# Four edits in the first attention of a three-block transformer kernel: the place of the dilated outputs, the way of the dilated values, the place of the norms, and four early gate tiles

## The reference

```
proj = h @ w_in[l]                       # h: rms_norm, scaled and shifted by c
qa, ka, va, qb, kb, vb, gates = split(proj)
qa, ka = rms_norm per head
o_a = neighbourhood_attention(qa, ka, va, rpb)        # 8 heads of 64
qb, kb = partial_rotary(rms_norm per head)
for g, (win, dil) in enumerate(((128,1),(512,4),(2048,16))):   # 3 groups of 4 heads
    o_g, lse_g = dilated_window_attention(qb[g], kb[g], vb[g], win, dil)
o_b = sum_g softmax(lse)[g] * o_g
gate_a, gate_b = split(sigmoid(gates + b_gate))
merged = gate_a * (o_a @ w_proj_a) + gate_b * (o_b @ w_proj_b)
x = x + gt1 * (merged @ w_o)
x = x + gt2 * swiglu(...)
```

## Time and profile before

| | |
|---|---|
| median of 3 runs | 3040.32 us |
| profiled execution | 3041.17 us |
| its span | 3038.6 us |
| mean granted clock | 0.958 of 2.4 GHz |
| PE busy | 2692.9 us, 89% |
| DVE, ACT, POOL busy | 1535.9, 1026.3, 1294.6 us |
| HBM traffic | 259 MB read, 3.15 MB written |

### The profile page before, as it was taken

The page is one execution under the profiler, slowest core; times in us unless marked ns, Lnnn a source line. Parts: engine busy times, 40 slices in busy tenths (PEclk is TensorE's granted clock), DMA queues, the critical chain, the costliest instruction groups (busy, mean ns, idle before and its releaser), DMA issues. The chain is left out here.

```text
span 3038.6 us, 37066 instructions
## 1 busy us (share of the span) xinstructions
PE 2692.9 (89%) x14304; PEld 2183.0 (72%) x14304; DVE 1535.9 (51%) x2279; ACT 1026.3 (34%) x1739; POOL 1294.6 (43%) x654
## 2 busy tenths in 40 slices
PE   1799669989999788888789999998799999699998
PEld 1587447868888565665578888886787888578886
DVE  2423424655445524555675555555577686632223
ACT  2333323232222433333431221113455555432222
POOL 2335554444444445555623333333344444344443
PEclk9899879999999899999999999998899999799999
DMA  5423222433334200000023333331111111022221
GB/s 193 150 93 114 98 79 101 148 125 130 132 133 138 69 29 15 25 18 15 35 98 124 119 125 112 118 111 53 49 42 63 43 56 49 35 83 97 97 97 70
DMA packets 78526, 264.53 MB, mean 87 GB/s; under 512 B 8464, under 2 KB 12688, under 8 KB 78352
## 3 DMA queue, kind: packets, MB, share of 16 engines
q1 hardware_dynamic: 70416, 248.67, 23.4%
q10 hardware_dynamic: 7648, 12.19, 1.3%
q0 software_dynamic: 288, 1.31, 0.1%
HBM read 258.99 MB, written 3.15 MB: 86 GB/s over the span
## 5 line engine op out<-in xcount | busy, mean ns | idle before, releaser
L1916 POOL TENSOR_TENSOR SLO<-RAW,SHI 128x1024 fp32r<-128x1024 f32 (+1 forms) x336 | 816.0, 2430 | 1215.7 <-ACT SHI L1754 1215.6
L1754 ACT ACTIVATE SHI<-RAW 128x1024 fp32r<-128x1024 f32 (+1 forms) x336 | 346.5, 1034 | 1199.9 <-PE PS L2175 1166.1
L2173 PE MATMUL PS<-HLh,SHI 128*128 128x512 f32 x1680 | 686.6, 409 | 24.3 <-DVE HLl L1985 15.2
L2174 PE MATMUL PS<-HLl,SHI 128*128 128x512 f32 x1680 | 659.6, 393 | 0.0
L2175 PE MATMUL PS<-HLh,SLO 128*128 128x512 f32 x1680 | 659.2, 392 | 0.0
L2173 PEld LDWEIGHTS PS<-HLh,SHI 128*128 128x128 f32 x1680 | 318.6, 190 | 118.4 <-issue 41.7
L2173 PE MATMUL PS<-hh,SHI 128*128 128x512 f32 (+1 forms) x944 | 352.8, 374 | 19.3 <-DVE hl L2065 9.9
L2175 PEld LDWEIGHTS PS<-HLh,SLO 128*128 128x128 f32 x1680 | 317.9, 189 | 69.1
L2174 PEld LDWEIGHTS PS<-HLl,SHI 128*128 128x128 f32 x1680 | 319.2, 190 | 65.2 <-issue 7.5
L2174 PE MATMUL PS<-hl,SHI 128*128 128x512 f32 (+1 forms) x944 | 347.0, 368 | 0.0
L2175 PE MATMUL PS<-hh,SLO 128*128 128x512 f32 (+1 forms) x944 | 346.9, 367 | 0.0
(11 more groups left out here) (227 smaller groups left out, 3957.0 us busy)
## 6 DMA issues: line engine op xcount, KB each, us to landing
RAW<-in_k_w SPq DMA_DIRECT2D x316, 512.0 KB, 3.2
ADA<-in_k_w SPq DMA_DIRECT2D x132, 512.0 KB, 4.1
early<-in_k_w SPq DMA_DIRECT2D x12, 512.0 KB, 10.7
RAW<-in_k_w SPq DMA_DIRECT2D x20, 256.0 KB, 2.7
XL<-in_xT ACTq DMA_DIRECT2D x1, 2048.0 KB, 12.4
bi<-in_k_bias ACTq DMA_DIRECT2D x16, 128.0 KB, 2.2
out<-XL SPq DMA_DIRECT2D x8, 256.0 KB, 2.1
bi<-in_k_bias ACTq DMA_DIRECT2D x8, 192.0 KB, 3.2
```

The costliest lines, as they stand in the source:

```text
L1754: eng.activation(u.hi, u.w, ACT.Copy).then_inc(S["a_hi"], 1)
L1916: eng.tensor_tensor(u.lo, u.w, u.hi.bitcast(F32), ALU.subtract).then_inc(S["g_lo"], 1)
L2173: eng.matmul(st.out, lh, rh, start=st.first and j == 0, stop=False)
L2174: eng.matmul(st.out, lh, rl, start=False, stop=False)
```

## The change

1. The dilated outputs of group j = 0 lie in XC behind c1 (high and low part), those of j = 1 on c1; only the latter wait for tile 47 (`[mtok(0, 47)] if j else []`).
2. The dilated values are computed with tokens side by side (`lhs_nat`), written to a scratch tensor in HBM (`v4`), and read back with every fourth token on its place (`dl_turned`, one job or two later). Both DMAs go out on ScalarE's queue; the values' token is now that of the read.
3. The tails of q and k start one yield later, and mark themselves as emitted two yields later.
4. Four gate tiles of the merge's first column pair (`early_gate`) stand at the end of the dense list: a projection and a copy to an f cell. The f ring changes places with pt, so that those cells stay untouched while the merge's buffers are laid out. In the merge, for p = 0, the sigmoid reads the copy.

In the diff, line numbers of the kernel after are up to 37 higher than those of the profile.

```diff
--- before.py
+++ after.py
@@ -834,15 +834,15 @@
 
     W = arena({"va": (1, 4 * 512, F32, 4), "qa": (4, 512, F32, 4), "vb": (1, 3 * 4 * 256, F32, 4),
                "qb": (6, 512, F32, 4), "mk": (1, 1536, F32, 4), "bi": (5, 384, F32, 4), "e": (4, 384, F32, 4),
-               "pt": (2, 768, F32, 4), "f": (4, 512, F32, 4), "r": (2, 512, F32, 4),
+               "f": (4, 512, F32, 4), "pt": (2, 768, F32, 4), "r": (2, 512, F32, 4),
                "m": (8, 8, F32, 4)}, [])
     qb2 = [place(f"qb2_{i}", [128, 512], F32, AR + 2048 * i)[:, :] for i in range(6)]
     oah = place("oah", [128, 4 * NT], F32R, HCh_at)
     oal = place("oal", [128, 4 * NT], F32R, HCl_at)
-    obh = place("obh", [128, 2 * NT], F32R, XC_at)
-    obl = place("obl", [128, 2 * NT], F32R, XC_at + 4096)
+    obs = [[place(f"ob{n}{j}", [128, NT], F32R, XC_at + (4096, 0)[j] + 2048 * i)[:, :] for i, n in enumerate("hl")]
+           for j in range(2)]
     oa = [(oah[:, NT * k:NT * k + NT], oal[:, NT * k:NT * k + NT]) for k in range(4)]
-    ob = [(obh[:, NT * k:NT * k + NT], obl[:, NT * k:NT * k + NT]) for k in range(2)]
+    ob = [tuple(o) for o in obs]
     oa_rdy, ob_rdy = [[] for _ in range(4)], [[] for _ in range(2)]
     MK = W["mk"].cells[0].ap
     stage = place("mstage", [128, 4224], F32, AR)
@@ -915,9 +915,6 @@
     def lhs_nat(i, k):
         return hl[k][0][:, 128 * i:128 * i + 128], hl[k][1][:, 128 * i:128 * i + 128], hl_rdy[k]
 
-    def lhs_dl(i, k):
-        return hl[k][0][:, i:NT:4], hl[k][1][:, i:NT:4], hl_rdy[k]
-
     qa_cells, qb_cells = {}, {}
 
     def na_qk(j, which):
@@ -930,10 +927,12 @@
 
         def tail():
             views = ("p (c r) -> p c r", "p (r c) -> p c r")
+            yield
             c.rdy = [headnorm(sq, b, b.ap, t, NT, gq8 if which == "q" else col("gka"), W, c.ap, c.free, views)]
             qa_cells[(which, j)] = c
+            yield
+            yield
             emitted.add(f"{which} {j}")
-            yield
 
         yield
         return tail()
@@ -994,6 +993,20 @@
 
     vb = W["vb"].cells[0].ap.rearrange("p (g t n) -> p g t n", g=3, t=4)
     vb_tok = []
+    v4 = [nc.dram_tensor(f"v4_{g}", [NT, 256], F32, kind="Internal").ap() for g in range(3)]
+    v4_tok = {}
+
+    def dl_values(g):
+
+        toks = []
+        yield from vproj("w_in", 1536 + 1536 + 256 * g, 4, lhs_nat, lambda i: vb[:, g, i, :], toks, vn_read)
+        v4_tok[g] = dma("act", v4[g].rearrange("(t p) n -> p t n", p=128), vb[:, g], toks)
+
+    def dl_turned(g):
+
+        vb_tok.append(dma("act", vb[:, g], v4[g].rearrange("(p t) n -> p t n", t=4), v4_tok[g]))
+        return
+        yield
 
     def dl_qk(j, g, which):
         u = getunit("w_in", ktiles(0, 8), seg((1536 if which == "q" else 1536 + 768) + 256 * g + 128 * j, 128))
@@ -1058,13 +1073,30 @@
     def dl_make(it, b, t_mm):
         j, r = it["j"], it["r"]
         ob_rdy[j] += out_split(b, t_mm, b.ap[:, 0:128], ob[j][0][:, r:NT:4], ob[j][1][:, r:NT:4],
-                               [mtok(0, 47)])
+                               [mtok(0, 47)] if j else [])
 
     for g in range(3):
         for w_ in ("q", "k"):
             qb_cells[(w_, g, 0)] = W["qb"].cells[2 * g + (w_ == "k")]
 
     run(bgz(pipelined([na_qk(0, "q"), na_qk(0, "k")])))
+    gated = {}
+
+    def gate_proj(m, off, W):
+        u = getunit("w_in", ktiles(0, 8), seg(3840 + 128 * (off + m), 128))
+        b = take()
+        t, = yield from proj(u, 0, [(b.ap, hl, hl_rdy, b.free)])
+        release(u, t)
+        return b, t, W["f"].next()
+
+    def early_gate(q, off):
+
+        b, t, sg = yield from gate_proj(q, off, W)
+        t1 = tick("a_vcopy")
+        put(VCopy("a", sg.ap, b.ap, t, sg.free, t1))
+        give(b, t1)
+        gated[(q, off)] = (sg, t1)
+        yield
 
     def qb2_cells():
         na_done = all_now()
@@ -1081,12 +1113,14 @@
     dense = []
     for j in range(1, 4):
         dense += [after(f"na {j - 2} scored")] if j > 1 else []
-        dense += [na_qk(j, "q"), na_qk(j, "k")]
-        g = j - 1
-        dense += [vproj("w_in", 1536 + 1536 + 256 * g, 4, lhs_dl, lambda i, g=g: vb[:, g, i, :], vb_tok, vn_read)]
-    dense += [dl_qk(0, g, w) for g in range(3) for w in "qk"]
+        dense += [na_qk(j, "q")]
+        dense += [dl_turned(j - 2)] if j > 1 else []
+        dense += [na_qk(j, "k"), dl_values(j - 1)]
+    dense += [dl_qk(0, 0, "q"), dl_turned(2), dl_qk(0, 0, "k")]
+    dense += [dl_qk(0, g, w) for g in (1, 2) for w in "qk"]
     dense += [after("na 3 done"), qb2_cells()]
     dense += [dl_qk(1, g, w) for g in range(3) for w in "qk"]
+    dense += [early_gate(q, off) for q in range(2) for off in (0, 8)]
     dense += [some(bg, 32)]
     first_out = lambda it, b, t: (na_make if "t" in it else dl_make)(it, b, t)
     weave((attention(heads, W, first_out), 0.6), (bgz(pipelined(dense)), 1.0))
@@ -1105,14 +1139,17 @@
             for q in range(2):
                 for off in (0, 8):
                     m = 2 * p + q
-                    u = getunit("w_in", ktiles(0, 8), seg(3840 + 128 * (off + m), 128))
-                    b = take()
-                    t, = yield from proj(u, 0, [(b.ap, hl, hl_rdy, b.free)])
-                    release(u, t)
-                    sg = W["f"].next()
+                    b = None
+                    if p == 0:
+                        sg, t = gated[(q, off)]
+                        src = sg.ap
+                    else:
+                        b, t, sg = yield from gate_proj(m, off, W)
+                        src = b.ap
                     t1 = tick("a_gate")
-                    put(Gate(b.ap, sg.ap, col("bg", off + m), t, sg.free, t1))
-                    give(b, t1)
+                    put(Gate(src, sg.ap, col("bg", off + m), t, sg.free, t1))
+                    if b:
+                        give(b, t1)
                     sgs[(q, off)] = (sg, t1)
                     yield
             for off, src, nk, o, ord_ in ((0, "w_proj_a", 4, oa, oa_rdy), (8, "w_proj_b", 2, ob, ob_rdy)):
```

## The result

The changed kernel takes 2996.64 us (median of 4 runs, 2988.56 to 3000.66), the kernel before 3040.0 in the same comparison: ratio 0.985, interval [0.983, 0.988]. It is 43.4 us faster; 77 were forecast. 2996.6 lies 3.6 us outside the range of 2948 to 2993. Two single executions of later runs, 7911 us (e4_gates) and 9089 us (best_w50_7), are left out of every median here. The profiled execution took 2998.94 us, of which 2994.7 is the span.

A forecast was written before the change was run, and what follows sets the result against it. TensorE, busy 89% of the span, was taken to bound the kernel. Gains less costs summed to 77.1 us, taking 3041.2 us to 2964.1, stated as 2964, with a range from 2948 to 2993.

The forecast's parts named there:

- (1): First dilated group: outputs beside c remove TensorE's 25.69 us stall; gain 26.5 us, bounds 20 and 30.
- (2): Dilated value projections: 288 matmuls with side-by-side weights gain 32.8 us; round trips cost 0, less cover 2 us.
- (3): Attention's q and k norms, further from scores: waits shortened by 6, 3.3 and 2 us, clock gain 5 us.
- (4): Second dilated group: four gate tiles fill TensorE's waits; gain 8.5 us, bounds 3 and 14.
- (5): Merge's start: TensorE waits 3.3 us for a late weight split; cost 5 us, bounds 0 and 9.
- behind the merge: Work after the merge: same order but for some coefficient tiles, none forced in a row; 0 us.
- three terms of waits: Attention norms: scores waiting for `qa` gain 6 us, head sums waiting for squares 3.3, first head sum of q 2.
- fourth term of (3): Attention: shorter waits leave less TensorE work at half clock; gain 5 us, bounds 0 and 7.
- term for less cover: Attention: shorter value projections leave less work between a score and its transposes; cost 2 us, bounds 0 and 15.
- (A): Rival: value projections get no shorter; 2997 us, or 2980 with half of the gain; chance 0.14.
- (D): Rival: the forced run of coefficient tiles only moves to the second dilated group; 25 us return, 2989 us; chance 0.02.
- signs set out for a wrong forecast: Value projections' pace over 0.2 us, TensorE's attention waits over 45 us, or clock from 120 us to merge under 0.85.

The follow-up runs named there:

- e4_gates: Kernel before with only the four gate tiles moved into the second dilated group; 3042.42 us, ratio 0.9998.
- best_w50_7: Changed kernel with six PSUM banks, read-back in the next job, sigmoids at their products, attention share 0.5, coefficient tile every 7th merge step; 2965.74 us.
- e2_values: Kernel before with only the dilated values from side-by-side weights, turned through HBM; 3021.96 us, ratio 0.9935.
- e3_norms: Kernel before with only the tails of q and k starting one step later and marked two later; 3041.83 us, ratio 0.9995.
- b_before: Kernel before with six PSUM banks in rotation instead of four until the last neighbourhood scores, nothing else; 3038.42 us, ratio 0.9986.
- b_norms: Kernel before with the later tails of q and k and six PSUM banks in rotation instead of four; 3025.56 us, ratio 0.994.
- a_less_norms: Changed kernel without the later tails of q and k (norms as before); 3002.84 us, ratio 0.987.
- b_banks: Changed kernel with six PSUM banks in rotation instead of four until the last neighbourhood scores; 2984.31 us, ratio 0.981.
- n_trip: Changed kernel without the six DMAs of the round trips through HBM, so part of the result differs; 2995.38 us.
- m1_turned: Changed kernel with each read-back from HBM issued at the head of the next projection's job, not in an empty job; 2993.93 us, ratio 0.9835.
- e1_outputs: Kernel before with only the first dilated group's outputs beside c, without the wait for coefficient tile 47; 3020.35 us, ratio 0.993.

## Why the prediction was wrong, step by step

| step | forecast | alone | inside the changed kernel |
|---|---|---|---|
| (1) outputs beside c | 26.5 | 23.0 | |
| (2) values | 32.8 - 2 | 23.2 | |
| (3) norms, with the clock's 5 | 16.3 | 2.3 | 6.5 |
| (4) gates in the second group | 8.5 | 7.0 | 8.4 |
| (5) merge's start | -5 | -8.6 | -7.4 |
| behind the merge | 0 | | -7.0, again -5.3 |

The first four rows are attention stretches: of the edit alone against before, or of the changed kernel without the edit against it (324.5 - 318.0 and 326.4 - 318.0). They were forecast at 82.1 us and gave 57.3. The column "alone" holds for (2) and (3) the shorter stall too, 7.1 and 4.7 us. What the traces say of TensorE's waits in the attention, in us:

| run | all waits | the stall | all others |
|---|---|---|---|
| before | 65.2 | 25.7 | 39.5 |
| e2_values | 68.7 | 18.6 | 50.1 |
| e3_norms | 63.9 | 21.0 | 42.9 |
| b_before (six banks) | 62.2 | 23.1 | 39.0 |
| b_norms (edit 3, six banks) | 53.3 | 20.5 | 32.8 |
| a_less_norms | 45.4 | 0 | 45.4 |
| after | 45.0 | 0 | 45.0 |
| b_banks (after, six banks) | 37.1 | 0 | 37.1 |

(3) is the step that failed: its three terms of waits, 6 + 3.3 + 2 = 11.3 us. In the changed kernel edit 3 changed TensorE's waits by 0.4 us (45.4 to 45.0), and alone it made those outside the stall 3.4 us longer. The 24 value matmuls that now stand between head sum and scores were there as forecast, and the waits for `qa` and for the square did go. But I asked only what the waiting instruction reads, not where it writes. A norm that starts later keeps its projection's bank longer, and of four banks the next free one is then the one just being emptied by the output split. Alone, edit 3 brought the waits for `oal` from 0.6 to 8.3 us, and 2.5 for `qa` at transposes. Two more banks bring its gain from 2.3 to 8.8 us (b_norms against b_before), and turn its 3.4 us of longer waits outside the stall into 6.2 of shorter ones. The Trainium skill, page "Perfetto Trace Analysis", section "Optimization Strategy", says that a gap that keeps coming back on the busiest engine can mean too few buffers in SBUF or PSUM; here the trace agrees, with three waits of 1.86 us at 166.14, 206.34 and 246.56 us.

The fourth term of (3), 5 us for the clock, was right in size for the changed kernel: busy time fell by 6.0 us with edit 3 there. Alone it fell by 1.0 us only. I had taken each microsecond at half clock as half a microsecond lost, and on matmuls with stride 4 nothing is lost (0.235 against 0.233 us); the term holds only together with edit 2. Of the 11.3 us of waits, even six banks brought only 6.2, and the waits for e grew by 3.8 us (2.5 to 6.3).

(2) was right on TensorE's pace, on the stride (32.9 us for 32.8) and on the round trips (n_trip). Its term for less cover, 2 us with bounds 0 and 15, was mis-sized, and this miss is as large as that of (3): alone, the waits outside the stall grew by 10.6 us. The largest part isn't cover: the waits for the square grew by 4.9 us and those for the normalised f by 2.2, where behind the empty job the rest of the tail of q is written in a row. I had read the order of the head sum of k, at the one place shown, and not that of q in the later rounds. In the changed kernel this costs 5 us of waits for the square (by m1_turned), which only the six banks turn into time. The waits for `oal` are 2.1 us of the 10.6.

(1) was near: 23.0 for 26.5, since the second group's scores wait 4.8 us longer (e1_outputs). (4) was right in the attention. (5) was right on the wait (3.07 for 3.3) and a little short on what is around it: 2.3 us more of busy time in the merge (the granted clock is 0.91 and 0.92 from 450 to 470 us) and 1.7 us longer to the norm. With the tiles behind the merge, edit 4 as a whole was forecast to bring 3.5 us and costs 4.2 (2995.27 against 2991.07).

"none of them is forced in a row: 0", said of the work behind the merge, was wrong. I had looked for forced runs and not at the norms, where one tile more in VectorE's order is paid in full. Of 7.0 us, 3.8 (2.4 and 1.4) are these tiles; the other 3.2 lie within the 1.0 to 6.1 us that six traces with the same instructions there show, and stay unattributed.

Of the rivals, (A) and (D) fell with the trace, and 2997 came about by other means than (A) says. Of the signs set out for a wrong forecast one was there, barely: over 45 us of waits in the attention (47.5: 321.8 us from 119.4 to 441.2 less 274.3 busy). And of the signs of a right one the plainest was missing: the last dilated values start at 440.9 us, not near 418.

## What to carry to other kernels

When an instruction moves, follow its buffer as well as its data: each step that now starts later holds its PSUM bank longer, and with few banks in rotation the wait comes back under another name. If background work is placed by counting steps, moving steps moves that work too; look for it ahead of the next norm, where everything else is waited for. And test edits both ways, alone and taken out of the whole: an edit tried beside a stall can shorten the stall and look useful (4.7 us here), and a sum of parts that agrees with the whole proves nothing by itself.
